# Useless products in the head, full-height spreads and quarter loads around the expert stream

## What is computed

```python
h = layer_norm(x, ln_in_g, ln_in_b)
# mixer: one input projection (2048 -> 5120), three small mixers, one output projection (2048 -> 2048)
mix = hybrid_mixer(h, w_in, conv_a, gate_ws, ..., w_out)
h = layer_norm(ALPHA * h + mix, ln1_g, ln1_b)
# MoE: 8 groups of 4 experts, the best group, the best two experts inside it
ffn = sum over the two chosen experts e of gate[t, e] * ((silu(h @ w1[e]) * (h @ w3[e])) @ w2[e])
out = layer_norm(ALPHA * h + ffn, ln2_g, ln2_b)
```

## Time and profile before

| | us |
|---|---|
| median of 3 runs | 1318.96 (1318.79 to 1319.05) |
| the profiled execution | 1318.82 |
| its span, first to last instruction | 1317.1 |

### The profile page before, as it was taken

How to read it: one execution, slowest core, us unless ns; L and a number is a source line. 1 busy time by engine, 2 the same in 40 slices (tenths; PEclk the granted TensorE clock), 3 DMA queues, 4 the chain that set the end, 5 groups by cost and what they waited for, 6 DMA issues and landing times.

```text
span 1317.1 us, 15734 instructions
## 1 busy us (share of the span) xinstructions
PE 1245.7 (95%) x6894; PEld 719.8 (55%) x6894; DVE 436.1 (33%) x622; ACT 314.1 (24%) x529; POOL 10.8 (1%) x18
## 2 busy tenths in 40 slices
PE   5999999999999999999999999999899999999984
PEld 5989999988754444444444434434444443434431
DVE  7788895755341102111020111102020111102027
ACT  6344333533421121111221111111211111111201
POOL 2000000000000000000000000000000000000000
PEclk8999999999999999999999999999999999999997
DMA  8565554596879999999999999999999999999993
GB/s 283 189 211 181 172 191 162 179 341 248 317 313 396 379 424 429 427 427 428 428 427 428 427 427 427 427 428 428 427 427 428 427 427 428 428 427 427 428 391 134
DMA packets 68393, 472.31 MB, mean 359 GB/s; under 512 B 7666, under 2 KB 8242, under 8 KB 40930
## 3 DMA queue, kind: packets, MB, share of 16 engines
q1 hardware_dynamic: 67890, 470.47, 88.1%
q10 hardware_dynamic: 432, 0.79, 0.2%
HBM read 469.14 MB, written 2.10 MB: 358 GB/s over the span
## 4 chain that ended last, share of the span: by engine, by line
PE 74%; DMA 22%; DVE 2%; ACT 0%; SPq 0%; issue 0%; DVEq 0%
PE psum L786 29%; PE psum L547 16%; DMA ring<-in_w_dram 11%; DMA slot<-in_w_dram 11%; PE psum L574 8%; PE psum L716 7%; PE psum L825 6%; PE psum L750 2%; PE psum L751 2%; PE psum L864 1%; PE psum L773 1%; PE psum L693 1%; DMA area_a<-in_x_dram 1%; DVE area_b L1716 0%; DVE area_b L1711 0%; PE psum L513 0%
## 5 line engine op out<-in xcount | busy, mean ns | idle before, releaser
L786 PE MATMUL psum<-ring,area_c 128*64 128x512 f32 x1536 | 456.8, 602 | 22.0 <-DMA ring<-in_w_dram 11.5
L786 PEld LDWEIGHTS psum<-ring,area_c 128*64 128x64 f32 x1536 | 137.5, 138 | 231.6 <-issue 229.9
L825 PE MATMUL psum<-ring,area_d 128*64 128x512 f32 x688 | 203.2, 594 | 9.0 <-ACT area_d L1135 6.1
L547 PE MATMUL psum<-in_high,w_high 128*128 128x256 f32 x576 | 164.7, 286 | 4.1 <-DVE in_low L1240 4.1
L1611 DVE TENSOR_TENSOR area_a<-area_a,psum 128x512 f32<-128x512 f32 x60 | 41.3, 688 | 382.3 <-PE psum L751 380.7
L1115 ACT ACTIVATE area_c<-psum,gain 128x128 f32<-128x128 f32 x256 | 96.5, 461 | 296.7 <-PE psum L716 296.7
L547 PE MATMUL psum<-in_low,w_high 128*128 128x256 f32 x576 | 163.9, 285 | 0.0
L547 PE MATMUL psum<-in_high,w_low 128*128 128x256 f32 x576 | 163.9, 285 | 0.0
L1255 DVE TENSOR_TENSOR w_low<-ring,w_high 128x2048 fp32r<-128x2048 f32 x56 | 128.4, 2293 | 80.9 <-ACT w_high L962 80.9
L962 ACT ACTIVATE w_high<-ring 128x2048 fp32r<-128x2048 f32 x56 | 107.3, 1916 | 163.9 <-PE psum L547 96.3
L716 PEld LDWEIGHTS psum<-one_hot,area_b 128*128 128x128 f32 x1024 | 119.5, 195 | 13.1 <-issue 12.2
(11 more groups left out here) (186 smaller groups left out, 1008.5 us busy)
## 6 DMA issues: line engine op xcount, KB each, us to landing
ring<-in_w_dram SPq DMA_DIRECT2D x126, 2048.0 KB, 25.7
slot<-in_w_dram SPq DMA_DIRECT2D x21, 2048.0 KB, 28.7
area_g<-in_w_dram SPq DMA_DIRECT2D x21, 2048.0 KB, 24.3
ring<-in_w_in_dram SPq DMA_DIRECT2D x40, 1024.0 KB, 5.0
ring<-in_w_dram SPq DMA_DIRECT2D x26, 1024.0 KB, 8.4
ring<-in_w_out_dram SPq DMA_DIRECT2D x16, 1024.0 KB, 5.2
slot<-in_w_dram SPq DMA_DIRECT2D x6, 1024.0 KB, 6.5
area_g<-in_w_dram SPq DMA_DIRECT2D x6, 1024.0 KB, 9.2
```

Source lines behind the costliest of these rows:

```text
L547: mm = pe.matmul(o[:, c, :], w[a][:, k, c * P:(c + 1) * P], in_part[b][:, kk, :], start=kk == 0 and a + b == 0 and c % 2 == 0, stop=kk == ...
L786: mm = pe.matmul(psum[i * CAP:(i + 1) * CAP, j // UNITS, :], gathered[:, kk, i * CAP:(i + 1) * CAP], w[i][:, k, :], start=kk == 0, stop=kk ...
L825: mm = pe.matmul(psum[i * CAP:(i + 1) * CAP, 4 + c, :], hidden_t[:, f, i * CAP:(i + 1) * CAP], w[i][:, c, :], start=f == 0, stop=f == FT - 1)
```

## The change

Head: `keep_clock(5, 4)` puts five products of `ones` with `slot_no` (256 columns) into PSUM bank 4 ahead of the transposes, and `keep_clock(4, 0)` puts four into bank 0 behind them; nothing reads them. Transition: `spread_rows` uses all 128 rows of `router_w`, with 128 rows of the identity's column (so all other rows are multiplied by zero); gather 3 of step 0 stands behind unit 2 instead of unit 1, spread 2 right behind it, and spread 3 behind block f = 1 of the hidden rows, in bank 0; DVE does `scaled_x1(3)` behind `hide`. Queue: `SPLIT_FILLS` is 32, so halves 20 to 31 come in quarters, and halves 182 to 187 come in quarters too, first quarters of a pair first, with semaphores of their own for the second quarters. End: two combines of step 14 stand between the wide columns of the last step.

The diff, cut to its core:

```diff
@@ constants @@
-    SPLIT_FILLS = 20
+    SPLIT_FILLS = 32
...
+        LATE = STEP_UNITS * PAIRS - SLOTS - 2
...
+        SPREAD_BANKS = (6, 4, 6, 0)
@@ sp @@
-            refills += [((EXTRA + SLOTS + 1,), EXTRA + 1), ((EXTRA + SLOTS + 2, EXTRA + SLOTS + 3), EXTRA + 2)]
+            refills += [((EXTRA + SLOTS + 1,), EXTRA + 1)]
+            refills += [((m, m + 1), m - SLOTS) for m in range(EXTRA + SLOTS + 2, SPLIT_FILLS, 2)]
...
+            def load_pair(m, j, pair):
+
+                for r in range(2):
+                    for i in range(2):
+                        sp.dma_start(quarter_of(m + i, r), half_matrix(j + i, pair)[:, r * D:(r + 1) * D]).then_inc(
+                            loaded[slot_of(m + i)] if r == 0 else second_rows[(m - LATE) // 2], 16)
+
+            unit_used(PAIRS - 2, SLOTS - 2)
+            load_pair(LATE, SLOTS - 2, PAIRS - 1)
+            for j in range(0, SLOTS // 2, 2):
                 last_unit_used(j)
-                load_expert_unit(LAST + SLOTS + j, SLOTS + j, PAIRS - 2)
+                load_pair(LAST + SLOTS + j, SLOTS + j, PAIRS - 2)
@@ pe, head @@
+            def keep_clock(n, bank):
+                for _ in range(n):
+                    pe.matmul(psum[:, bank, 0:2 * TT * CAP], ones[:], slot_no[:].rearrange("p t s -> p (t s)"),
+                              start=True, stop=True)
+            keep_clock(5, 4)
             turn_rows(normed, 0)
             pe.wait_ge(ln_chan_ready, 1)
             turn_rows(normed, 1)
+            pe.wait_ge(h_cm_ready[0], 1)
+            keep_clock(4, 0)
@@ pe, spread_rows @@
-                    one_row = ident[0:2 * NC, r * NC + c:r * NC + c + 1].to_broadcast([2 * NC, P])
-                    mm = pe.matmul(psum[:, b + r, :], one_row, rows_1, start=True, stop=True)
+                    one_row = ident[:, r * NC + c:r * NC + c + 1].to_broadcast([P, P])
+                    mm = pe.matmul(psum[:, b + r, :], one_row, router_w[:, 0:CW], start=True, stop=True)
@@ pe, arrived @@
+                elif LATE <= m < LATE + 6:
+                    pe.wait_ge(second_rows[(m - LATE) // 2], 16 * 2)
@@ pe, unit_products @@
+                    if j == (2 if first else 1):
                         pe.wait_ge(slot_gates_kept, it + 1)
                         gather(it, s, 3)
+                        if first:
+                            spread_rows(2)
                     if behind and 2 <= j < 2 + NC:
                         combine(it - 1, j - 2)
-                    if first and 3 <= j < 5:
-                        spread_rows(j - 1)
@@ pe, step @@
                 for f in range(FT):
                     hidden_rows(f, arrived(STEP_UNITS * it + 2 * UNITS + f))
+                    if first and f == 1:
+                        pe.wait_ge(gt_drained, 1)
+                        spread_rows(NC - 1)
@@ pe, last_two_steps @@
-                for c in range(NC):
-                    combine_apart(a, c)
+                combine_apart(a, 0)
+                combine_apart(a, 1)
...
+                    if f < 2:
+                        combine_apart(a, 2 + f)
@@ dve @@
-                    for c in range(NC):
+                    for c in range(NC - 1):
                         scaled_x1(c)
-                    dve.wait_ge(x1_ready, NC)
...
                 hide(it, it == PAIRS - 1)
+                if it == 0:
+                    scaled_x1(NC - 1)
+                    dve.wait_ge(x1_ready, NC)
```

More of the change, by code:

```diff
@@ L227, in hybrid_layer @@
         loaded = [sem(f"expert_half_loaded{i}") for i in range(SLOTS)]
+        second_rows = [sem(f"late_second_quarters_loaded{i}") for i in range(3)]
         extra_loaded = sem("extra_half_loaded")
@@ L400, in _ @@
             refills = [((m, m + 1), m - EXTRA - 1) for m in range(EXTRA + 1, EXTRA + SLOTS, 2)]
-            refills += [((EXTRA + SLOTS + 1,), EXTRA + 1), ((EXTRA + SLOTS + 2, EXTRA + SLOTS + 3), EXTRA + 2)]
+            refills += [((EXTRA + SLOTS + 1,), EXTRA + 1)]
+            refills += [((m, m + 1), m - SLOTS) for m in range(EXTRA + SLOTS + 2, SPLIT_FILLS, 2)]
             for both, held in refills:
                 for r in range(2):
-                    unit_used(0, held, r)
+                    unit_used(held // STEP_UNITS, held % STEP_UNITS, r)
                     for m in both:
@@ L410, in _ @@
                 load_expert_unit(m, m % STEP_UNITS, m // STEP_UNITS)
-            for j in range(SLOTS):
+            for j in range(SLOTS - 2):
                 unit_used(PAIRS - 2, j)
                 load_expert_unit(LAST + j, j, PAIRS - 1)
-            for j in range(SLOTS // 2):
+            def load_pair(m, j, pair):
[6 more added lines that the diff above has]
+            for j in range(0, SLOTS // 2, 2):
                 last_unit_used(j)
-                load_expert_unit(LAST + SLOTS + j, SLOTS + j, PAIRS - 2)
+                load_pair(LAST + SLOTS + j, SLOTS + j, PAIRS - 2)
             def load_columns(m, at, i, f, first, end, signal):
@@ L682, in spread_rows @@
             def spread_rows(c):
-                b = 6 - 2 * (c % 2)
+                b = SPREAD_BANKS[c]
                 if c == 0:
@@ L688, in spread_rows @@
                     pe.wait_ge(logits_fixed, 1)
-                else:
-                    pe.wait_ge(x1_ready, c - 1)
+                elif c == 2:
+                    pe.wait_ge(x1_ready, 1)
                 for r in range(2):
-                    one_row = ident[0:2 * NC, r * NC + c:r * NC + c + 1].to_broadcast([2 * NC, P])
-                    mm = pe.matmul(psum[:, b + r, :], one_row, rows_1, start=True, stop=True)
+                    one_row = ident[:, r * NC + c:r * NC + c + 1].to_broadcast([P, P])
+                    mm = pe.matmul(psum[:, b + r, :], one_row, router_w[:, 0:CW], start=True, stop=True)
                 mm.then_inc(rows_spread, 1)
@@ L840, in step @@
                 if first:
-                    pe.wait_ge(x1_ready, NC)
+                    pe.wait_ge(x1_ready, NC - 1)
                 else:
@@ L845, in step @@
                     hidden_rows(f, arrived(STEP_UNITS * it + 2 * UNITS + f))
+                    if first and f == 1:
+                        pe.wait_ge(gt_drained, 1)
+                        spread_rows(NC - 1)
+                if first:
+                    pe.wait_ge(x1_ready, NC)
             def step_again(i2, s):
@@ L895, in last_two_steps @@
                         last_rows(f, c, [wide[i][:, f, c, :] for i in range(2)], s_wide)
+                    if f < 2:
+                        combine_apart(a, 2 + f)
                 for f in range(FT):
+                    if f == 0:
+                        pe.wait_ge(y_drained, NC * b)
                     if f == FT - 1:
```

## The result

The changed kernel takes 1309.18 us (median of 4 runs, 1308.77 to 1311.79), beside 1319.01 before (4 runs, 1318.79 to 1320.11): a ratio of 0.9928, with an interval of 0.9911 to 0.9945. The profiled execution took 1308.77 (span 1307.1), 10.05 less than the one before. The head's clock fell in the trace as rival (a) says.

What follows compares the result with a forecast made beforehand. The prediction took the expert-weight stream to bound the kernel from about 460 us; its terms, -2.4 - 3.9 + 1.6 - 2.9 + 1.0 - 5.1 + 0.5, gave -11.2 and a forecast of 1307.7 us, range 1304.0 to 1312.0.

Steps and rivals of the forecast that it cites:

- rival (a): Head: the clock falls all the same, before or just after 22.27 us, giving 1309.4 to 1310.1; chance 0.23.
- What bounds the kernel: From about 460 us the stream of expert weights sets the time, 428 GB/s over 778 us; PE only follows.
- head: Before the input projection: nine unused products keep PE's clock full, removing the half-clock stretch from 22.27 to 27.14; -2.4 us.
- transition: Spreads ahead of the first expert product: 128 rows in place of eight keep the clock full; -3.9 us.
- gather 3 behind unit 2: Step 0: unit 2 now waits for ACT to drain gather 2, and the weight queue runs empty; +1.6 us.
- quarters to load 31: Stream after the first step: earlier quarter loads close gaps, -2.9 us, against a lower quarter rate, +1.0.
- rate of the end's quarters: End of the weight stream: three more pairs loaded at the quarters' rate cost 0.5 us.
- the end: After the last w2 data: less work remains, -3.5 us, and combines between wide columns wait less, -1.6; together -5.1.
- three terms of the stream: Weight stream: gather 3 behind unit 2 (+1.6), quarters to load 31 (-2.9 and +1.0), rate of the end's quarters (+0.5).
- partial result: Head: about -0.7 us if the clock stays up at 20.3 but falls again shortly after PE has restarted.
- Rival (d): Weight stream: quarters do not keep their rate; at 332 GB/s the kernel gets slower, 1331.6 us; chance 0.02.
- Rival (c): End: last columns come later than PE needs, or combines still wait; 2 us less gain, 1309.7; chance 0.12.

Runs made afterwards that it cites:

- e3_gather_back: The changed kernel with gather 3 of step 0 back behind gather 2, spread 2 left behind unit 2: 1306.12 us.
- e10_best: e3_gather_back with six and eight products in the head, and one product each ahead of and behind the transition's rank products: 1305.89 us.
- e6_split20: The changed kernel with SPLIT_FILLS back at 20, so halves 20 to 31 load whole again: 1311.74 us.
- e8_end_undone: The changed kernel with halves 182 to 187 whole and the four combines of step 14 in a row again: 1313.31 us.
- e2_spread_only: The kernel before with only the spreads changed from 8 to 128 rows: 1317.29 us.
- e1_head_only: The kernel before with only the nine products in the head: 1318.31 us beside 1318.69.
- e7_clock8: The changed kernel with eight products instead of four behind the transposes, thirteen in all: 1308.75 us.
- e11_fill: The changed kernel with only two added products in the transition, around the rank products: 1308.8 us.
- e4_rows8: The changed kernel with the spreads back at 8 rows: 1312.19 us.

## Why the prediction was right or wrong

**What bounds the kernel: right.** The stream is whole for 774 us at 427 GB/s, and gains ahead of it reach the end: in the trace the first expert product came 4.19 us earlier (369.34 to 365.15), the release by the last w2 data 5.13, the end of the last product with weights 10.02.

The sum, term by term, with what the traces show:

| term | forecast | measured | from |
|---|---|---|---|
| head | -2.4 | -0.5 (-0.7 in the block, +0.2 a later start; the start lies between 21.55 and 22.68 in the 13 profiles) | 25.41 to 24.75, 22.27 to 22.46 |
| transition | -3.9 | -3.7 | second column, 321.66 to 317.94 |
| gather 3 behind unit 2 | +1.6 | +1.7 | e3_gather_back, e10_best |
| quarters to load 31 | -1.9 | -2.6 | e6_split20 |
| rate of the end's quarters | +0.5 | +0.75 | e8_end_undone |
| the end | -5.1 | -4.9 | fourth column, 29.64 to 24.75 |

The three terms of the stream give -0.15, and the third column shows -0.9 (mean of three kernels with the old loads, 897.5, against five with the new, 896.6). The remaining 0.75 is open; the moved spread 3 and the way that the terms act on each other were not tried.

**The head: the size was wrong, and the step that failed** is "I take -2.4, because [...] waits of that length hardly ever cost the clock". The rows behind it were of another stretch, in which PE had run for hundreds of us; in the head it had not, though no run shows that this is why. Nor did those rows promise so much: the mean of 0.99 hides three falls of 3.4 us in the trace of before (at 764, 942 and 1119 us), and e2_spread_only and e8_end_undone lost the clock in the transition, where PE's two waits were 0.8 us each. Of nine profiles with nine products three kept the clock (23.26 or 23.27 us for the block) and six lost it around the end of the idle time of 2.78 us, for 24.74 to 24.76 us in five and 25.98 in one (e8_end_undone, where it fell at 21.2, before PE started again): 24.4 in the mean. The two profiles without the products had 25.41 and 24.75. So the nine products are worth about 0.7 us by the profiles and 0.4 by the medians of e1_head_only, neither clear of nothing; it is also the size that the forecast gave as the partial result and then did not take. The two profiles with 13 and 14 products both kept the clock, after 1.05 us of idle time in each. That looks like the cure, but three kernels with nine kept it too, after 2.78, and the medians of e7_clock8 and of e11_fill, with its nine products in the head, do not differ (1308.75, 1308.8). So it is a suspicion, not shown. Why the clock falls in one run and not in the next, with the same instructions, stays open as well.

The prize was too large besides. The forecast took 4.9 us at half clock as 2.4 lost, since "at full clock the same products take half of it". They take 0.12 us for 0.21, so 4.9 us at half clock cost 2.15, as the blocks of 25.41 and 23.26 show. By the same rates the 1.5 us that the half clock was shorter are 0.65, and the block became 0.66 shorter.

In the prediction the Trainium skill was cited ("TensorE: Matmul & The Clock Gate", Part 4: PE-mode transpose) for the rule that transposes do not bring the full clock. The traces disagree again: in the changed kernel the clock rose at 15.8, in the middle of the transposes, and in e2_spread_only, where only one small transpose at 6.4 us stands ahead of them, at 16.3. Windows of PE alone in that trace, in which PE does nothing but transposes from 12.17 to 17.88:

```profile
15.00:16.00 1.00, 1.00 (x6) 1.00 1.06 391
16.00:17.00 1.00, 1.00 (x10) 1.00 1.05 385
```

**Gather 3: right.** The wait is there as forecast (1.6 us, on ACT), and the queue is the sufferer: 384 GB/s in place of 421, and 417 once it is undone. By the medians the price is higher: 2.9 us between e11_fill and e10_best on one chip and 2.6 between e7_clock8 and e3_gather_back on another. The head's longer cover does not account for it, as it is worth nothing that could be told. The runs of one kernel spread over 1.2 to 2.4 us here, so whether gather 3 costs more than the 1.7 of the traces stays open.

**Quarters: right in sign, worth 0.7 more than forecast.** Their rate was sized well, 421 GB/s and 0.9 us for 12 halves at 0.076. The gaps closed more completely than I had followed: 2.6 net and 0.9 of rate are 3.5, not 2.9, gross. Rival (d) is dead by the same run, since even 144 halves at that rate cost 10.9.

**The end: right.** -4.9 for -5.1. Rival (c) did not come: PE waited for no column, and the one wait of a combine is 0.3 us.

Had the head been put at its partial result, the sum would have been 1309.4, 0.2 from what was measured. That closeness is in part luck: the other terms are off by 0.1 to 0.7 each, with both signs, and 0.75 us more were gained that no term holds.

## What to carry to other kernels

Put the small steps of a transition on all 128 rows where zeros are at hand: it cost PE nothing here, and the clock that it kept was worth 3.7 us, as much as the two spreads themselves take. Do not take a gain of clock from waits in another stretch of the kernel: read it at the place itself, in several profiles, and forecast the partial result. And before a gather is moved so that a unit starts sooner, ask who drains its input; here the unit waited the whole 1.6 us, the DMA queue ran short for it, and the change was better without that step: 1306 in place of 1309 us.

## What the runs showed that was not expected

- In the transition the clock depended on how many rows the products use: it fell to half, 1.2 GHz, under a busy PE and for 10.24 us in three of three profiles with 8 rows, and never for that long in ten with 128 rows.
- The same kernel gets the same instructions at different clocks: the full clock first came between 10.2 and 16.9 us in the head, and the falls of a few us came in some profiles and not in others. The moment of the rise does not decide it: with the same nine products e8_end_undone rose at 11.0 and fell, e4_rows8 rose at 11.2 and did not. e2_spread_only lost in the end (1.6 us) part of what it had gained in the transition.
- Loads of 1 MB in place of 2 MB run 1.5% slower, 421 for 427 GB/s over more than 770 us, though the DMA share is 1.01 in both; splitting pays only where the queue would otherwise stand empty.
